# A two-layer transformer on one core: layer 0's join in another order, four weight slabs moved

## The reference

```
for l in range(2):
    sh1, sc1, g1, sh2, sc2, g2 = split(silu(c) @ w_ada[l] + b_ada[l], 6)      # latent
    csh1, ..., cg2             = split(silu(c_ctx) @ w_ada[l] + b_ada[l], 6)  # context
    h_lat = rms_norm(x, norm1_g[l]) * (1 + sc1) + sh1        # the same for ctx
    y_lat, y_ctx = parallel_mixer(h_lat, h_ctx, w_in[l], ...)
    x = x + g1 * y_lat                                       # ctx too in layer 0
    f = grouped_moe(norm and modulate (ctx, x), w_router, w_gate[l], w_up[l], w_down[l])
    x = x + g2 * f                                           # ctx too in layer 0
return rms_norm(x, final_g)
```

## Time and profile before

| | us |
|---|---|
| median of 3 executions | 1592.64 |
| lowest, highest | 1592.12, 1596.81 |
| profiled execution: span | 1594.1 |
| PE busy | 1438.2 (90%) |
| DVE, ACT, POOL busy | 854.5, 651.0, 241.1 |
| layer 0's experts on PE | 595.5 to 889.5 |

### The profile page before, as it was taken

One profiled execution on the slowest core, in us unless ns is written; L12 is line 12 of the kernel. 1 busy time (PEld: TensorE's weight loads), 2 busy tenths in 40 slices (PEclk: granted clock), 3 DMA queues, 4 the chain that ended last, 5 costly groups with the idle time before them and its releaser, 6 DMA issues.

```text
span 1594.1 us, 17062 instructions
## 1 busy us (share of the span) xinstructions
PE 1438.2 (90%) x6672; PEld 1003.1 (63%) x6672; DVE 854.5 (54%) x1112; ACT 651.0 (41%) x887; POOL 241.1 (15%) x210
## 2 busy tenths in 40 slices
PE   3999999989999859999999689899889978998884
PEld 1786667546888637888888478765568864433332
DVE  3577973865644448888888357870860142111103
ACT  2654443345323257777777265430340122111112
POOL 0007951400000011111110200660500000000000
PEclk8999999999999969999999889999999999999998
DMA  9511107790142437999999861116343456999992
GB/s 355 216 53 53 54 32 211 277 378 1 53 158 97 168 132 276 400 399 399 401 401 393 298 226 53 54 53 157 135 183 123 141 213 252 393 394 393 395 393 74
DMA packets 167146, 352.14 MB, mean 221 GB/s; under 512 B 21776, under 2 KB 22928, under 8 KB 167056
## 3 DMA queue, kind: packets, MB, share of 16 engines
q1 hardware_dynamic: 162880, 335.72, 57.8%
q0 software_dynamic: 3456, 12.58, 2.2%
q10 hardware_dynamic: 720, 2.62, 0.4%
HBM read 339.38 MB, written 11.53 MB: 220 GB/s over the span
## 4 chain that ended last, share of the span: by engine, by line
PE 77%; DVE 8%; DMA 5%; POOL 4%; ACT 3%; issue 3%; SPq 1%; DVEq 0%; ACTq 0%; POOLq 0%
PE bank L1324 7%; PE bank L744 4%; PE bank L1346 4%; PE bank L1082 4%; PE bank L1076 4%; PE bank L1073 4%; PE bank L628 4%; DMA ring<-in_w_ada 2%; PE bank L663 2%; PE bank L891 2%; PE bank L896 2%; PE bank L1101 2%; PE bank L1106 2%; PE bank L1111 2%; PE bank L893 2%
## 5 line engine op out<-in xcount | busy, mean ns | idle before, releaser
L2858 DVE TENSOR_TENSOR slab_lo<-slab,high 128x4096 fp32r<-128x4096 f32 x48 | 211.9, 4418 | 7.1 <-ACT high L2000 6.3
L2000 ACT ACTIVATE high<-slab 128x4096 fp32r<-128x4096 f32 x48 | 174.4, 3637 | 22.0 <-PE bank L1082 14.7
L1324 PE MATMUL bank<-narrow_slab,picked 128*64 128x512 f32 x256 | 114.4, 601 | 12.1 <-issue 11.8
L2283 POOL DMA_INDIRECT feed_rows<-token_table,slot_token x16 | 41.0, 2561 | 489.4 <-DVE slot_token L2798 290.8
L1325 PE MATMUL bank<-narrow_slab,picked 128*64 128x512 f32 x256 | 114.6, 602 | 0.0
L744 PE MATMUL bank<-hT,ring 128*128 128x512 f32 (+1 forms) x256 | 104.6, 547 | 0.0
L1324 PEld LDWEIGHTS bank<-narrow_slab,picked 128*64 128x64 f32 x256 | 34.7, 138 | 82.9 <-issue 82.4
L3022 DVE TENSOR_TENSOR hidden<-bank,gated 64x512 f32<-64x512 f32 x16 | 11.1, 694 | 119.5 <-ACT gated L2155 119.5
L1848 ACT ACTIVATE gsig<-bank 128x512 f32<-128x512 f32 (+1 forms) x32 | 15.7, 491 | 141.2 <-PE bank L628 71.5
L628 PE MATMUL bank<-hT,ring 128*128 128x256 f32 x320 | 72.9, 383 | 0.0
L2243 POOL TENSOR_TENSOR pair<-pf 128x512 f32<-128x512 f32 (+1 forms) x32 | 34.4, 1076 | 222.7 <-DVE pb L2479 216.3
(11 more groups left out here) (353 smaller groups left out, 3033.8 us busy)
## 6 DMA issues: line engine op xcount, KB each, us to landing
ring<-in_w_ada SPq DMA_DIRECT2D x24, 2048.0 KB, 13.6
ring<-in_w_in SPq DMA_DIRECT2D x24, 2048.0 KB, 9.4
slab<-in_w_gate SPq DMA_DIRECT2D x16, 2048.0 KB, 14.1
slab<-in_w_up SPq DMA_DIRECT2D x16, 2048.0 KB, 14.1
slab<-in_w_down SPq DMA_DIRECT2D x16, 2048.0 KB, 13.9
narrow_slab<-in_w_gate SPq DMA_DIRECT2D x16, 2048.0 KB, 18.1
narrow_slab<-in_w_up SPq DMA_DIRECT2D x16, 2048.0 KB, 22.1
narrow_slab<-in_w_down SPq DMA_DIRECT2D x16, 2048.0 KB, 19.2
```

The source lines that it names most:

```text
L1324: T.matmul(bank[0][0:64, :], x, gate[:, k, :], start=(k == 0), stop=(k == KT - 1))
L2000: S.activation(half_of(e, kind)[:], w[:], ACT.Copy)\
L2858: V.tensor_tensor(low[:], w[:], half_of(e, kind)[:].bitcast(f32), ALU.subtract)\
```

## The change

1. `w_ada` slabs 16 to 19 move in `loads` from behind the experts to ahead of them, into the lanes 0 to 3. PE works out their rows (`ada_rows`) as the first thing in `dealt_experts`, and turns them behind GATE of expert 0. GATE of expert 0 is issued ahead of slab 18.
2. `LANE` changes: UP of even experts goes to lane 4 (outside the ring), DOWN of odd ones to lane 0. So expert 0's GATE and UP lie outside the ring; GATE 1, DOWN 0, UP 1 and DOWN 1 go, in this order, to lanes that held slabs 17, 18, 19 and 16.
3. Behind the experts `refill` loads `("in", 1, 3)` to `("in", 1, 6)`; layer 1's lane order changes to fit, and the wait for all gathers goes.
4. The join takes tiles 2, 3, 0, 1. The latent segment's adds, squares, sums, root, norm and modulation go first; the context's adds, squares and norm follow. `PAIRED` stays 12, so the pairs are the latent's eight and four of the context's.
5. The q projection of layer 1 puts two outputs in one bank and waits for the latent half of `h_ready` alone. In PE's order it stands behind both calls of `add_squares`.

```
-    LANE = ((5, 1), (0, 3), (2, 4))
+    LANE = ((5, 1), (4, 3), (2, 0))
...
-            if l == 1:
-                loads += ada_loads[16:20]
-                lane += range(SLOTS)
+            order = ((2, 0, 3, 1), (2, 1, 3, 0))[l]
...
+            if l == 0:
+                loads += ada_loads[16:20]
+                lane += range(SLOTS)
...            # PE, dealt_experts
+                    for n in range(16, 20):
+                        ada_rows(n, 4)
                     turn_rows(0)
                     by_high(0, GATE)
                     by_low(0, GATE)
+                    ada_turn(19, 4)
...            # PE, join_tokens
+                    for n, t in enumerate(LATE_TILES):          # (2, 3, 0, 1)
+                        pe.wait_ge(sem["tok_joined"], n + 1)
                         ... (eight transposes)
+                        if n == 2:
+                            add_squares(0, range(KT))
                     add_squares(1, range(KT))
...            # PE, after dealt_experts
-                    for n in range(16, 20):
-                        ada_rows(n, 4)
                     join_tokens()
-                    ada_turn(19)
...            # SyncE
-                if l == 1:
-                    for t in range(4):
-                        sp.wait_ge(sem[f"tok_there{t}"], 32)
+                    if loads[n] == ada_loads[18]:
+                        sp.wait_ge(sem["merged_ready"], 16)
+                        fill_slab(0, GATE)
...
-                    for e, kind in ((0, GATE), (0, UP), (1, GATE), (0, DOWN), (1, UP), (1, DOWN)):
+                    for e, kind in ((0, UP), (1, GATE), (0, DOWN), (1, UP), (1, DOWN)):
                         i = LANE[kind][e]
                         if i < SLOTS:
                             sp.wait_ge(*slot_spent[max(m for m in range(base) if lane[m] == i)])
...
-                    first_after = {i: slot_of(ada_loads[16 + i]) for i in range(SLOTS)}
+                    first_after = {lane[m]: m for m in map(slot_of, [("in", 1, x) for x in (3, 4, 5, 6)])}
...            # ScalarE, layer 1
+                    modulate(2, LATE_SEGS[:1], gain1[:, 1], mod[:, 1, 0:KT, :])
+                    late_squares(1)
+                    segment_std(1)
+                    near_high(0)
+                    near_high(1)
+                    modulate(2, LATE_SEGS[1:], gain1[:, 1], mod[:, 1, 0:KT, :], tile_high, 1)
...            # VectorE: join(0), join(1), join(2), add_late(0), join(3), and then in layer 1
+                    norm_late(0)
+                    add_late(1)
+                    norm_late(1)
                 for k in range(KT) if l else (KT - 1,):
                     tile_low(k)
```

More of the change, by code:

```diff
@@ L1658, in finish_norm, with modulate @@
                 if count:
-                    act.wait_ge(sem["normed_ready"], KT * count)
+                    act.wait_ge(sem["normed_ready"], normed_before(count))
                 S.activation(rstd[:, lo:TOK], result(key)[:, lo:TOK], ACT.Sqrt, scale=1.0 / D, bias=epsv[:, 0:1])\
                     .then_inc(sem["norm_std"], 1)
-            def modulate(count, lo, gain, shift, behind=None):
+            def modulate(count, segs, gain, shift, behind=None, part=0):
                 for k in range(KT):
-                    act.wait_ge(sem["normed_ready"], KT * count + k + 1)
-                    for sg in range(1 if lo else 0, 2):
+                    act.wait_ge(sem["normed_ready"], normed_before(count) + KT * part + k + 1)
+                    for sg in segs:
                         a = slice(sg * SEG, (sg + 1) * SEG)
@@ L1672, in modulate, with late_squares, segment_std @@
                         behind(k)
+            def late_squares(part):
+                sg = LATE_SEGS[part]
+                for k in range(KT):
+                    n = KT * part + k
+                    act.wait_ge(sem["tok_added"], n + 1)
+                    S.activation(square_late[:, n, :], xT[:, k, sg * SEG:(sg + 1) * SEG], ACT.Square)\
+                        .then_inc(sem["square_ready"], 1)
+            def segment_std(part):
+                key, sg = late_ms(part), LATE_SEGS[part]
+                act.wait_ge(*is_ready(key))
+                act.wait_ge(sem["normed_ready"], KT * 2)
+                S.activation(rstd[:, sg * SEG:(sg + 1) * SEG], result(key)[:, 0:SEG], ACT.Sqrt, scale=1.0 / D,
+                             bias=epsv[:, 0:1]).then_inc(sem["norm_std"], 1)
             def head_std(l, h, lo):
@@ L2024, in dealt_experts @@
                     split_high(0, UP)
+                    ada_keep(19)
                     keep_feed(0)
@@ L2050, in join_tokens @@
                 def join_tokens():
-                    ada_keep(19)
-                    for t in range(4):
-                        if t == 3:
+                    for t in LATE_TILES:
+                        if t == LATE_TILES[-1]:
                             S.activation(unused_std[:], epsv[:], ACT.Sqrt)
@@ L2392, in _, with add_late @@
                 ada_mod(n)
+            def add_late(part):
+                sg = LATE_SEGS[part]
+                dve.wait_ge(sem["tok_turned"], 2 * part + 2)
+                for d in range(KT):
+                    a = slice(sg * SEG, (sg + 1) * SEG)
+                    got = bank[4 * sg + d // 2][:, d % 2 * SEG:(d % 2 + 1) * SEG]
+                    V.scalar_tensor_tensor(xT[:, d, a], got, mod[:, 0, 5 * KT + d, 1 - sg:2 - sg],
+                                           xT[:, d, a], ALU.mult, ALU.add).then_inc(sem["tok_added"], 1)
             def add_scaled(key_bank, l, d, at_gate, lo):
@@ L2407, in _, with norm_late @@
                 segs = segs_of[l]
-                if l == 1:
-                    for sg in range(2):
-                        a = slice(sg * SEG, (sg + 1) * SEG)
-                        dve.wait_ge(sem["norm_std"], stds_before(2) + sg + 1)
-                        link(V.reciprocal(rstd[:, a], rstd[:, a]))
+                def norm_late(part):
+                    a, b = LATE_SEGS[part] * SEG, (LATE_SEGS[part] + 1) * SEG
+                    dve.wait_ge(sem["norm_std"], stds_before(2) + part + 1)
+                    link(V.reciprocal(rstd[:, a:b], rstd[:, a:b]))
+                    norm(2, a, b, None, part)
                 def tile_low(k):
@@ L2423, in row_low @@
                     V.tensor_tensor(low, w, high[:].bitcast(f32), ALU.subtract).then_inc(sem["way_low"], 1)
-                norm(2 * l, 0, None if l else tile_low)
-                if l == 1:
-                    ada_mod(19)
+                if l == 0:
+                    norm(0, 0, behind=tile_low)
+                else:
+                    norm_late(0)
+                    add_late(1)
+                    norm_late(1)
                 for k in range(KT) if l else (KT - 1,):
@@ L2872, in dealt_experts @@
                     rows_and_shares()
+                    ada_mod(19)
                     split_low(1, GATE)
@@ L2910, in join_tokens @@
                     join(2)
-                    add(0, range(3))
+                    add_late(0)
                     join(3)
-                    add(0, range(3, KT))
-                    add(1, range(KT))
                 def experts(ph):
```

122 lines of the change are left out of this document (54 added, 68 removed).

## The result

| | before | after |
|---|---|---|
| median of 6 executions each | 1596.3 us | 1609.7 us |
| lowest to highest | 1592.12 to 1598.39 | 1606.05 to 1612.39 |
| ratio of the two, 95% interval | | 1.0087 [1.0072, 1.0102] |
| profiled execution, span | 1594.1 | 1610.5 |

The changed kernel is slower by 13.9 us by the ratio, between 11.5 and 16.3. The forecast was +7.5 by its terms, +7.2 as stated: the sign was right, the size half of what came. Three of the six executions of the kernel before are those behind the 1592.64 that the forecast was added to, and the three newer ones took 1595.79 to 1598.39 us. The median is so 3.7 us higher, and the ratio is compared, not the bare time. Applied to 1592.64 the ratio gives 1606.5, which is also above the 1605 that the range ended at.

What follows compares the result with a forecast made beforehand. It took the expert loop as bound by PE and DMA engines, both full. Loop 5.5, store 1.3 and join 0.7 made +7.5 on 1592.6, 1600.1 us, stated as 1599.8; own range 1596.5 to 1603, 8-in-10 range 1591.5 to 1605.

Steps and rivals of the forecast that it cites:

- The moved rows: Ahead of the experts: rows of slabs 16 to 19 fit in PE's wait for the first feed rows, free on PE.
- The join's gain: Latent-first join: PE's order keeps the projection behind the context's sums, so no gain; +0.7 us (-1.5 to +3).
- Rival 1: Expert loop: run-ahead absorbs the late loads, no stall; warm start -1.9, join +2.0, total 1592.7 us; chance 0.18.
- Rival 2: No loop stall, and latent projection overlaps the context half: join -4.9, warm start -1.9, total 1585.8 us; chance 0.10.
- Rival 3: Loop stalls feed on each other, engines also idle: 9 us in loop, 3.3 in join, 1604.9; 0.16 with rival 4.
- Rival 4: Moved rows take 13.6 us at low clock and run into the first feed: +4 us; 0.16 together with rival 3.
- The store, +1.3 said: Last y_out store behind the experts shares the engines with the fourth w_in slab: +1.3 us (0 to 5.2).
- The loop, +5.5 said: Expert loop: four late slabs leave 6.0 us of DMA backlog, never made up; less 0.5 us margin, PE stalls 5.5.
- The warm start: First gate product of the experts runs at full clock after the moved rows, saving some 1.9 us; not in the sum.

Runs made afterwards that it cites:

- e3: The kernel before with only the changed kernel's latent-first join and layer 1 start, slabs and lanes untouched: 1598.91 us, ratio to before 1.0018.
- e7: The changed kernel with the remedies of e2 and e1, plus three of eight q projection slices ahead of the context's sums: 1592.53 us, ratio to before 0.9984.
- e5: The kernel before, with GATE 1, DOWN 0, UP 1 and DOWN 1 held until PE has turned the first feed rows: 1603.07 us, ratio to before 1.0069.
- e1: The changed kernel, with slab ("in", 1, 6) held until all gathers of the join have landed: 1604.94 us, ratio to before 1.0050.
- e4: The kernel before, with GATE 1, DOWN 0, UP 1 and DOWN 1 held until slot_token is read: 1600.4 us, ratio to before 1.0025.
- e2: The changed kernel, with the adaLN rows of slabs 16 to 19 computed earlier, in PE's routing gaps, so expert slabs issue sooner: 1598.83 us, ratio to before 1.0021.

## Why the prediction was half right

**What held.** The reading of the bound: a loop with the DMA engines full and PE full has no spare, so bytes that come late are paid. The moved rows did hide in PE's wait: they ended as the first feed turn began, at 596.12 against 595.54, and the gather itself had been issued 0.5 us later. The join's gain fell to PE's order, as the earlier trace rows had suggested: +0.7 said, +0.4 measured up to the near chunk; e3 and e7 show both sides of it. Rival 1 (the backlog is absorbed) falls with after and with e5. Rival 2 (the join overlaps as it is written) falls with e3; e7 reaches part of it by moving the projection. Rival 3 came nearer in time, +12.3, but not by its cause: its first link, f_acts_hi behind a late UP split, is there, yet the DMA engines never fell idle in the long stretch and the join cost 0.4, not 3.3. Rival 4 falls, since the rows took 9.01 us, not 13.6.

**The store, +1.3 said, +3.9 measured.** This is the term of the sum that was furthest off, by 2.6 us. I saw the fourth slab ahead of the store, but added only the store's own 0.52 MB once more, as if the two shared the engines evenly, and left the slab's bytes as the upper end, 5.2. They came whole: 2.10 MB at 0.400 MB/us are 5.2 us, e1 without the slab lands the store after 3.3, and 3.3 + 5.2 is the 8.5 of after. Against the kernel before it is 3.9, since there the slab issued 8.6 us ahead of the store, at 881.53, landed only after 12.0 us, at 893.5, beside the store (4.65).

**The loop, +5.5 said, +6.9 measured.** The kind of count was sound, as e4, after and e5 show. Two things were off. The rows took 9.01 us and started at 587.18, not 586.2, so the flow began at about 595.3 instead of 593.8: 1.5 us. The stall came only in part "in small pieces over the loop": 6.0 us fell on the first two turns, where GATE 1, UP 1 and GATE 2 are all late at once, and 3.3 us on five experts near the end. ScalarE waited for slabs from 605 on, not from 660. The warm start was rightly left out of the sum, but for the 0.3 us that I took off at the end: the late slabs took it back. So part of the loss is taken where the late slabs are first used and is then carried, and the rest comes when the loads have fallen behind by another margin.

**Layer 1, nothing said, +4.9 in this profile.** One stretch at a low clock, near 1018 in the kernel before, is 1.3 us longer in after. The rest is in the tail, 286.47 against 282.83. But e4, whose code is the same as before from the loop's end on, has 286.51, and the other kernels lie at 284.1 to 286.6: most of this is between executions, or before's profile had a short tail, the shortest of the nine. By the ratio some 2 us of the 13.9 (less the 11.6 that the near chunk shows) is left, in layer 1 or in how two single executions differ. Its cause stays open.

**The parts against the total.** Of the 6.4 us between 7.5 and 13.9 the store is 2.6, the loop 1.4, the later turn 0.6, the join and the gathers -0.4, and 2.2 are not found. By the ratios e2 takes back 0.66% (10.6 us), e1 0.37% (5.9 us), both together 0.82% (13.1 us). The two singly add to 16.5; each of these differences is uncertain by some 4 us, so I read it as agreement and no more.

## What to carry to other kernels

Before loads are moved toward a stage in which the DMA engines are full, count the bytes that are newly late against the spare until that stage; what is left over is paid, part of it at the first use and part when the later loads run out of margin, and here none of it was made up. Look which bulk load will be issued just ahead of a small transfer on which a chain waits, and hold it: here that took one wait and gave back 5 us at the store. e4, where nothing was held for it, lost 3.3 us at a gather beside four slabs. An overlap in the data does not exist until it is in each engine's order too; here three slices of a product had to be moved by hand.

## What the runs showed of the hardware

- A 0.5 MB store landed after 3.3 us without that slab (e1), 4.65 in the kernel before, and 8.5 with one 2 MB slab issued ahead of it on another engine's queue (after).
- The fourth of four slabs issued in a row has a long issue: SyncE's row at 597.73 lasts 9.34 us in after, at 586.18 11.48 in e4, against 0.37 for each slab from 600 to 740 in the kernel before, where the engines are full too. It grows as the loads fall behind: at 840.26 an issue takes 3.57 us in the kernel before. SyncE issues nothing else meanwhile; the next slab of after goes out at 607.11, where it was 605.97.
- 9 us of adaLN products raised the granted clock of 586 to 593 from 0.50 to 0.63 and had it at full by the first gate product: 2.09 us for the same eight matmuls instead of 3.75. By 634 the late loads had taken the gain back.
- A gather of rows issued within 1 us of four 2 MB slabs landed after 11.7 us in e4, and after 8.4 in the kernel before, where none ran beside it.
- After 2.42 us of waiting PE ran eight matmuls in 3.59 us, with a granted clock of 0.50 from 616 to 618 (after); after 1.73 us of waiting the same eight took 2.12 at 1.00 (before). e5 shows 3.59 us again, behind a wait of 1.91.
